# All norms' factors on ScalarE with one table set of logarithm and exponential, and a reordered gate of p's projection

## What is computed

```python
# first_block, per layer (AdaLN: mod = silu(c) @ w_ada + b_ada)
h = modulate(rms_norm(x, norm_mix[l]), sh1, sc1)
p = h @ w_in[l]                  # attention, rwkv, gmlp and gate columns
x = x + gt1 * (sum of sigmoid(gate_n) * (branch_n @ w_branch[l, n]) @ w_out[l])
h = modulate(rms_norm(x, norm_ffn[l]), sh2, sc2)
x = x + gt2 * conv_gated_ffn(h, ...)
# rwkv branch: decay = exp(-exp(-softplus(-(w0 + tanh(xw) @ w_up)) - 0.5)),
#   the wkv7 scan, a group norm with rsqrt(var + 64e-5), times sigmoid(xg) @ g_up
# after both layers: rms_norm(x, norm_final)

# second_block, per layer
h = x + 0.5 * swiglu(rms_norm_2(x, norm_ffn1[i]), ...)
u = rms_norm_2(h, norm_mix[i])   # -> q, k (each with its own rms norm), v, c, gates
h = h + (g_attn * y_attn + g_conv * y_conv) @ w_o[i]   # y_conv: conv, layer norm, silu
h = h + 0.5 * swiglu(rms_norm_2(h, norm_ffn2[i]), ...)
x = h + (p[i] @ w_pe_proj[i]) * sigmoid(rms_norm_2(h, norm_pe[i]) @ w_pe_gate[i])

def rms_norm(x, g):
    return x * lax.rsqrt(jnp.mean(x * x, axis=-1, keepdims=True) + 1e-6) * g
```

## Time and profile before

| | us |
|---|---|
| median of 3 runs (lowest to highest) | 2241.94 (2241.05 to 2243.96) |
| profiled execution, its own time | 2241.22 |
| span of its profile | 2239.4 |
| TensorE busy | 2190.3 (98%) |
| VectorE busy | 1700.1 (76%) |
| ScalarE busy | 1260.0 (56%) |
| mean granted TensorE clock | 0.994 |

### The profile page before, as it was taken

The page is one execution under the profiler, slowest core; times in us unless marked ns, Lnnn a source line. Parts: engine busy times, 40 slices in busy tenths (PEclk is TensorE's granted clock), DMA queues, the critical chain, the costliest instruction groups (busy, mean ns, idle before and its releaser), DMA issues.

```text
span 2239.4 us, 39411 instructions
## 1 busy us (share of the span) xinstructions
PE 2190.3 (98%) x16408; PEld 1990.9 (89%) x16408; DVE 1700.1 (76%) x2625; ACT 1260.0 (56%) x2094; POOL 12.4 (1%) x20
## 2 busy tenths in 40 slices
PE   7999999999999999999999999999999999999999
PEld 6798989998898987999888899888888889998888
DVE  7778469987786648877687669788678867878876
ACT  4754345554765435555566457665556554675653
POOL 0000000000000000000000000000000000000000
PEclk9999999999999999999999999999999999999999
DMA  9444455777644346555555533455545554245553
GB/s 384 164 161 164 167 193 185 277 243 262 229 151 166 135 154 227 197 172 187 179 189 191 188 129 123 168 200 191 188 166 188 188 188 151 106 159 206 189 188 132
DMA packets 116002, 415.67 MB, mean 186 GB/s; under 512 B 12736, under 2 KB 15936, under 8 KB 115312
## 3 DMA queue, kind: packets, MB, share of 16 engines
q1 hardware_dynamic: 115824, 413.15, 52.5%
HBM read 409.94 MB, written 3.16 MB: 184 GB/s over the span
## 4 chain that ended last, share of the span: by engine, by line
PE 81%; DVE 11%; ACT 5%; DMA 2%; issue 1%; SPq 0%; POOL 0%; DVEq 0%; ACTq 0%
PE bank L197 81%; DVE lo L204 3%; DVE arena L204 3%; ACT arena L244 2%; DVE arena L212 2%; DMA raw<-W 2%; ACT L244 1%; ACT hi L244 1%; PE bank L201 1%; DVE ada L221 0%; DMA arena<-WA 0%; DVE h L212 0%; DVE xT L212 0%; ACT h L244 0%; DVE sml L224 0%
## 5 line engine op out<-in xcount | busy, mean ns | idle before, releaser
L197 PE MATMUL bank<-h,hi 128*128 128x256 f32 (+1 forms) x5344 | 1227.5, 315 | 0.0
L244 ACT ACTIVATE hi<-raw 128x1024 fp32r<-128x1024 f32 x656 | 686.9, 1055 | 592.3 <-PE bank L197 523.5
L197 PE MATMUL bank<-h,lo 128*128 128x256 f32 x3440 | 989.5, 288 | 13.5 <-DVE h L204 6.6
L197 PEld LDWEIGHTS bank<-h,hi 128*128 128x128 f32 x5344 | 883.5, 191 | 66.7 <-issue 2.2
L204 DVE TENSOR_TENSOR lo<-raw,hi 128x1024 fp32r<-128x1024 f32 x656 | 793.2, 1220 | 95.7 <-ACT hi L244 94.2
L197 PEld LDWEIGHTS bank<-h,lo 128*128 128x128 f32 x3440 | 656.9, 191 | 28.6 <-DVE h L204 8.2
L197 PE MATMUL bank<-act,hi 128*128 128x512 f32 x1056 | 370.0, 393 | 0.0
L197 PE MATMUL bank<-act,lo 128*128 128x256 f32 x1056 | 294.7, 279 | 0.0
L197 PEld LDWEIGHTS bank<-act,hi 128*128 128x128 f32 x1056 | 197.9, 187 | 47.0
L197 PE MATMUL bank<-arena 64*64 64x64 f32 (+7 forms) x2994 | 224.7, 263 | 6.7 <-ACT arena L244 3.7
L197 PEld LDWEIGHTS bank<-arena 64*64 64x64 f32 (+3 forms) x2994 | 172.1, 146 | 41.6 <-issue 12.4
(11 more groups left out here) (149 smaller groups left out, 1920.1 us busy)
## 6 DMA issues: line engine op xcount, KB each, us to landing
raw<-W SPq DMA_DIRECT2D x664, 512.0 KB, 3.4
ada<-WA SPq DMA_DIRECT2D x80, 512.0 KB, 3.4
arena<-WA SPq DMA_DIRECT2D x16, 512.0 KB, 15.1
p_projected<-arena SPq DMA_DIRECT2D x2, 1024.0 KB, 8.6
arena<-scr SPq DMA_DIRECT2D x2, 1024.0 KB, 8.9
arena<-p_projected SPq DMA_DIRECT2D x2, 1024.0 KB, 4.9
xT<-x SPq DMA_DIRECT2D x2, 512.0 KB, 4.6
arena<-lora SPq DMA_DIRECT2D x2, 512.0 KB, 10.7
```

What stands on the lines that cost most here:

```text
L197: return self.done(lambda e: e.matmul(out, l, r, start=start, stop=stop, skip_group_check=True))
L244: return self.done(lambda e: e.activation(out, in_, f, scale=scale, **kw))
```

## The change

All norms take their factor on ScalarE: Ln of the mean square, then Exp of minus half of it into `rs_t`; for mx another Exp with bias log(0.5) gives the half factor in `var_t`, and pl gets that one alone. VectorE's reciprocals and halvings for norms go, and whoever waited for them waits for ScalarE. A new helper `table()` names the set that holds both Ln and Exp, and loads it at once: at the program's start, at the beginning of each group of updates, in rwkv's steps "length" and "centre", after conv2's Square, after the Square for q and k, and behind layer 0's ple. In ple VectorE makes the low part of h and adds the square one item later, behind the next `th` (new function `x_low`).

```diff
+    def table(self):
+        if self.e is not None:
+            self.e.preload_act_table_set("natural_log_exp_and_others")
...
-            def factor(norm):
-                v.wait_ge(a_main, ("sd", norm))
-                v.recip(rs_t, var_t).then_inc(v_main, ("rs", norm))
-            def half_factor(norm):
-                v.wait_ge(v_main, ("rs", norm))
-                v.ts(var_t, rs_t, 0.5, None, MUL).then_inc(v_main, ("half rs", norm))
...
             def normed(norm, l, shift, beside=()):
-                v.wait_ge(v_main, ("rs", norm))
+                v.wait_ge(a_main, ("rs", norm))
...
+                if kind != "ple":
+                    x_low(kind, l, m)
+            def x_low(kind, l, m):
+                norm, g, h, hl_ = next_norm(kind, l)
+                x = t256(xT, m)
                 if g:
                     v.wait_ge(a_main, ("h", norm, m))
                     v.wait_ge(v_main, ("x", norm, m))
...
-                    if m == 0:
-                        factor(norm)
-                        half_factor(norm)
                     th = ptmp[m % 2]
                     v.wait_ge(pe_main, item)
-                    v.wait_ge(v_main, ("half rs", norm))
+                    v.wait_ge(a_main, ("half rs", norm))
                     v.tt(th, ps(item)[:, 0:256], var_t, MUL).then_inc(v_main, ("ple th", l, m), frees=item)
+                    if m:
+                        x_low(what, l, m - 1)
                     v.wait_ge(a_main, ("ple th", l, m))
...
                     x_update(what, l, m, [th], None)
+                    if m == KD - 1:
+                        x_low(what, l, m)
...
-            def deviation(norm):
+            def factor(norm):
                 a.wait_ge(pe_main, ("stat", norm, 7))
-                a.act(var_t, statb[:, 0:256], ACT.Sqrt, bias=C("eps6")).then_inc(a_main, ("sd", norm), frees=("stat", norm))
+                a.act(var_t, statb[:, 0:256], ACT.Ln, bias=C("eps6")).then_inc(a_main, ("ln", norm), frees=("stat", norm))
+                a.wait_ge(a_main, ("ln", norm))
+                if norm[0] != "pl":
+                    a.act(rs_t, var_t, ACT.Exp, scale=-0.5).then_inc(a_main, ("rs", norm))
+                if norm[0] in ("pl", "mx"):
+                    a.act(var_t, var_t, ACT.Exp, bias=C("lhalf"), scale=-0.5).then_inc(
+                        a_main, ("half rs", norm))
...
             def updates(kind, l, p, nk):
                 if p == 0:
-                    a.act(sml[:, 192:193], C("one"), ACT.Sqrt).then_inc(a_main)
+                    a.table()
...
+                    elif what == "length":
+                        a.table()
...
                     elif what == "centre":
+                        a.table()
...
                         a.act(cy2, cyc, ACT.Square).then_inc(a_cv, ("csq", l))
+                        a.table()
...
                         a.act(sq, qr, ACT.Square).then_inc(a_main, ("qk sq", l))
+                        a.table()
...
                     if l < L - 1:
                         x_update(what, l, m)
+                        if m == KD - 1:
+                            a.table()
```

More of the change, by code:

```diff
@@ L62 @@
 PARC, NPAR = par_columns()
-CST = [("ident", 128), ("bo", 128), ("bom", 128), ("ones", 128), ("one", 1), ("mhalf", 1), ("eps6", 1), ("eps5", 1),
+CST = [("ident", 128), ("bo", 128), ("bom", 128), ("ones", 128), ("one", 1), ("mhalf", 1), ("lhalf", 1), ("eps6", 1), ("eps5", 1),
        ("epsg", 1), ("cos", 256), ("sin", 256),
@@ L103, in constants @@
     c["one"] = np.ones((128, 1))
-    for n, v in (("mhalf", -0.5), ("eps6", 1e-6), ("eps5", 1e-5), ("epsg", 64e-5)):
+    for n, v in (("mhalf", -0.5), ("lhalf", math.log(0.5)), ("eps6", 1e-6), ("eps5", 1e-5), ("epsg", 64e-5)):
         c[n] = np.full((128, 1), v)
@@ L1212, in tensor_program @@
                     take(ONE, item)
[L1213 removed]
+                    pe.wait_ge(a_main, ("rs", ("mx", q[0])))
                     for c in range(2):
@@ L1815, in vector_program @@
                     gain(("n2", l), l, 32, "norm_ffn")
-                    factor(("n2", l))
                     normed(("n2", l), l, shift2, () if l else (3, 6))
@@ L1831, in vector_program @@
                             v.tt(var_t, var_t, adab[:, 256:512], MUL).then_inc(v_main, "final var", frees="stat2")
-                            v.wait_ge(a_main, "final sd")
-                            v.recip(var_t, var_t).then_inc(v_main)
-                            v.wait_ge(v_main)
+                            v.wait_ge(a_main, "final factor")
                             v.tt(var_t, var_t, rs_t, MUL).then_inc(v_main, "final rs")
                         else:
-                            v.wait_ge(v_main, ("rs", norm))
+                            v.wait_ge(a_main, ("rs", norm))
                 elif what == "up":
@@ L1910, in vector_program @@
                         f.tiles(16)
-                        if m == 0:
-                            factor(("mx", l))
-                            half_factor(("mx", l))
                         v.wait_ge(pe_main, item)
-                        v.wait_ge(v_main, ("half rs", ("mx", l)))
+                        v.wait_ge(a_main, ("half rs", ("mx", l)))
                         if m >= 2:
@@ L2018, in start_factor @@
                 a.wait_ge(a_main, ("ln", norm))
-                a.act(rs_t, var_t, ACT.Exp, scale=-0.5).then_inc(a_main, ("rs", norm))
+                if norm[0] != "pl":
[3 more added lines that the diff above has]
+                        a_main, ("half rs", norm))
             def start_x(k):
@@ L2306, in scalar_program @@
             a.wait_ge(d_cst0, "cst0")
-            a.act(sml[:, 192:193], C("one"), ACT.Ln).then_inc(a_main)
+            a.table()
             late = later = None
@@ L2326, in scalar_program @@
                 elif what == "start":
-                    start_factor()
+                    factor(("n1", 0))
                     for k in range(KD):
@@ L2336, in scalar_program @@
                     f.slow = False
-                    deviation(norm)
+                    factor(norm)
                     a.wait_ge(v_ad, ("mod", l, 15))
@@ L2426, in scalar_program @@
                     l = q[0]
-                    deviation(("n2", l))
+                    factor(("n2", l))
                     a.wait_ge(v_ad, ("mod", l, 39))
@@ L2440, in scalar_program @@
                             ffn_shares(("f", *q, m))
-                        deviation(norm)
+                        factor(norm)
                         if norm == ("f1", 0):
                             a.wait_ge(v_main, "final var")
-                            a.act(var_t, var_t, ACT.Sqrt, bias=C("eps6")).then_inc(a_main, "final sd")
+                            a.act(var_t, var_t, ACT.Ln, bias=C("eps6")).then_inc(a_main, "final ln")
+                            a.wait_ge(a_main, "final ln")
+                            a.act(var_t, var_t, ACT.Exp, scale=-0.5).then_inc(a_main, "final factor")
                 elif what == "up":
@@ L2496, in scalar_program @@
                         if q[1] == 0:
-                            deviation(("mx", l))
+                            factor(("mx", l))
                     m = 3 if what == "c last" else q[1] - 1
@@ L2559, in scalar_program @@
                     if m == 0:
-                        deviation(("pl", l))
+                        factor(("pl", l))
                     a.wait_ge(v_main, ("ple th", l, m))
```

6 lines of the change are left out of this document (1 added, 5 removed).

## The result

| | before | after |
|---|---|---|
| median of the 4 runs shown with the result | 2241.51 | 2227.38 |
| lowest to highest | 2241.05 to 2243.96 | 2226.15 to 2231.66 |
| profiled execution | 2241.22 | 2228.34 |
| span of its profile | 2239.4 | 2226.6 |

The ratio is 0.9934, with a 95% interval of 0.9922 to 0.9946: 12.1 to 17.5 us faster, where 10.7 were forecast. The direction and the chain of reasons held; the size did not. The median lies 0.4 us inside the low end of the range and the lower two of the four runs lie outside it.

What follows compares the result with a forecast made beforehand. TensorE, busy 2190.3 of 2239.4 us, was taken as the bound, so only its waits counted. Terms -0.9 - 4.2 + 1.4 + 1.1 - 0.7 - 2.4 - 5.0 = -10.7 us gave 2231, range 2227 to 2236.5.

Steps and rivals of the forecast that it cites:

- What bounds the kernel: TensorE, busy 2190.3 of 2239.4 us; time saved on ScalarE or VectorE counts only where TensorE waits for it.
- ple: Gate of p's projection, layer 0: VectorE's item falls from 4.23 to about 3.1 us; wait and half clock go, -5.0 us.
- Decay: Both layers: one load moves to an idle stretch, one goes; TensorE's waits at 94.06 and 611.94 shrink, -4.2 us.
- Mix: Layer 0: a new load between weight split and Tanh lengthens TensorE's wait at 54.28, +1.4 us.
- Conv2: Both layers: load delays copy `ysh` at no cost; one load ahead of the Silu goes, -2.4 us together.
- Centre: Both layers: two loads added on ScalarE delay the path to waits such as 1.47 at 339.00, +1.1 us together.
- n1: Norm n1 of layer 1: factor comes 1.3 us earlier, shortening TensorE's wait of 0.81 us, -0.9 us.
- q and k: Both layers: Ln and Exp share a set; of two loads leaving the path one returns close to it, -0.7 us.
- A: Rival: ple's half clock stays or a later h tile limits; only 1 to 2.5 of 5.0 left, 2234 to 2235; chance 0.12.
- B: Rival: decay's gain doesn't carry to TensorE; half to all of 4.2 lost, 2233 to 2235; chance 0.10.
- C: Rival: loads on a busy ScalarE cost twice 1.30 at mix and each centre, +3.9 together, 2235; chance 0.04.
- D: Rival: named loads stand on TensorE's path, replaced ones did not; only ple gains, +6.8, 2249; chance 0.04.

Runs made afterwards that it cites:

- before_ple2: The kernel before with ple's new order alone (low part of h and its square one item later), factors as before: 2237.29 us, ratio 0.9975.
- before_decay: The kernel before with the table() in rwkv's step "length" alone, nothing else changed: 2235.65 us, ratio 0.9974.

## Why the prediction was right and wrong

*What bounds the kernel*: right. Only waits of TensorE and its clock moved the time; two loads more and ten us more of ScalarE did no harm.

*ple*: right, -5.0, by the mechanism named (the 3.03 us item, the bank freed in time). Of its two parts, the half clock was no separate gain.

*Decay*: the mechanism was right; the term was sized at 2.1 a layer and is 2.5 to 2.7, because a TENSOR_SCALAR of the right shape was taken for the instruction that the Ln waits for. The second load stood ahead of the first Exp and not of an Ln, which changes no number.

*Mix*: +1.4 was the wait alone. The later Tanh measured +1.7, and the longer half-clock stretch of the first profile 1.0.

*Conv2*: the step "That fits with 1 us to spare, so it costs nothing" failed. It followed the delayed copy to its reader on TensorE and not to what stands behind its reader on VectorE.

*Centre*: ScalarE's delay was right (0.45 for 0.5), but in layer 0 it cost TensorE nothing, and the wait of 1.47 that was to grow by it does not hang on this chain: it stays even when the Exp comes 1.8 us sooner. The 1.1 us gained there come from loads of raw that land sooner, which kernels without any edit at centre show too. *n1, q and k*: right in kind, 0.1 to 0.8 for 0.9 and 1.2 for 0.7.

*The step that failed the size* is the clock, above all behind the decays. The forecast gave it 1.7 us, within the ple term ("most of the rest the half clock behind it"), and nothing at any other wait that was removed, as if a half-clock stretch belonged to the one wait beside which the one profile shows it. The two waits of decay were priced by their length alone, 4.2 us. Taking them out or putting them back moved the mean time by 5.7 (±1.0) and 7.9 (±1.3) us, of which 2.8 and 3.0 are the clock's share. Over all executions the share fell by 4.0 (±1.2) us. At ple the place gives 5.0 with and without a half-clock stretch beside it. For the single terms more than that is not shown: the share came out lower with mix's shorter wait (2.0 ±2.2) and higher with conv2's and centre's (2.2 and 2.0, ±1.4 and 1.5). Why the clock is lowered less often stays open.

The low end of the range, 4 us below the forecast, was set for waits that shrink further on, and not for the clock. That the median still lies inside it, by 0.4 us, is luck. Without the clock the sum stood: 10.7 forecast, 10.5 in the rest. That too is partly luck, for the errors of single terms nearly cancel (+0.3 mix's wait, +1.3 conv2, +0.1 to 0.8 n1, against -0.9 decay, -0.5 q and k, -1.5 to -2.2 centre).

None of the rivals came: A and B by the waits that are gone, C by the 1.29 us from the load's start at 54.12 to the Tanh, and D since its gains did not stay away, though two of its prices came true: mix cost its load in full (1.5 for 1.4) and `ysh` too (1.23 for 1.3 in each layer), while centre and q and k hardly cost.

## What to carry to other kernels

Count the loads of function tables by what waits behind them, not by their number: naming a set that holds both functions pays where one follows the other in a chain (decay: 2.5 to 2.7 us a layer for one load fewer and one moved), and costs its full time where a function of another set comes next and nothing covers it (mix). When a load or any instruction is put ahead of a copy, go on from the copy's readers to the instructions behind them on their engines. Before a gain is put down to the edit beside it, look whether a kernel without that edit has it too. And where single profiles differ by stretches of a lower clock, compare mean clock and time over many executions before putting a stretch down to the edit.

## What the runs showed that was not expected

The changed kernel's executions differ by up to 9.4 us (2224.4 to 2233.8), and time multiplied by the mean clock is constant to about 2 us. In the kernel before it is not. In the profiles the half-clock stretches last 3.41, 6.83 or 10.24 us and come again at four places: near 222 and 750 us in all 13 profiles, both in the middle of full work, near 54 and 890 in 11 of 13 each, behind waits. Three more stand behind waits that the change removes: at 94 in `before_ple2`, at 1666 in the first profile of before and at 1661 in `before_decay`. Their length differs between executions. Removing two waits of 2 us lowered the clock's share by about 3 us in both kernels in which it was tried, with standard errors of 1.0 and 1.4. What at these places brings the clock down was not tried.

The load of 512 KB behind that of ada at centre, layer 0, takes 5.8 to 6.8 us to land in three of the 13 profiles, 4.1 to 4.3 in eight, and 5.2 and 5.6 in the two whose load at centre was moved. The cause is open.
